# A decoder step's cross-attention: the samples' softmaxes done earlier, and the sums of squares in four column groups

## The chip, the cores and the metric

The kernel is one program on one core of a Trainium2 chip. The metric is device time in microseconds (us) of one execution. Names of engines: PE is TensorE (matmuls and transposes), DVE is VectorE, ACT is ScalarE, POOL is GpSimd, SP is SyncE, which here only issues DMAs. PEld is PE's weight load. All data are float32.

## What is computed

Two layers of a decoder run for 256 prompt tokens (one sequence) and 32 sample tokens (8 sequences of 4 tokens), 288 tokens in all, with 1024 features. Each layer is three sub-layers, each followed by `x <- LN(ALPHA*x + f(x))`: a mixer (block-sparse attention with a convolution in layer 0, a gated spatial unit in layer 1), cross-attention over 256 memory tokens, and 16 experts of which each token takes two. What the change touches is the cross-attention and the layer norm:

```python
def layer_norm(x, g, b):
    mu = jnp.mean(xf, -1, keepdims=True)
    var = jnp.mean(jnp.square(xf - mu), -1, keepdims=True)
    return (xf - mu) * lax.rsqrt(var + LN_EPS) * g + b

def cross_attn(x, mk, mv, wq, wo):          # 4 heads of 256 features
    q = (x @ wq).reshape(B, L, H_X, HD_X)
    s = jnp.einsum('blhd,bmhd->bhlm', q, mk) * (HD_X ** -0.5)
    p = jax.nn.softmax(s, axis=-1)
    o = jnp.einsum('bhlm,bmhd->blhd', p, mv).reshape(B, L, D_MODEL)
    return o @ wo
```

The prompt's memory keys and values are computed from `mem_prompt`, and are outputs too. Each of the 8 sample sequences has keys and values of its own, read from a cache in HBM (2 MB per unit of four sequences and half the data, 8 units in a layer).

## The kernel before

Tokens lie along the free dimension: a feature tile is 128 partitions by 288 tokens, eight of them a tensor. The work of every engine is written out by hand in one order, and semaphores tie the engines together. A table, `tile_order()`, lists every tile that PE writes into the four general PSUM banks (`acc`) and who empties it ("v" DVE, "s" ACT; a capital letter marks the first half of a pair copied at once). A tile's bank is its place in that table modulo 4, and PE may write it when the tile four places earlier has been emptied (`bank_free`). Three further tiles of PSUM stand outside: `psS` (scores), `psV` and `psN` (value products). SP loads 2 MB units into a ring of six slots; a unit is loaded when the one that had its slot has been read.

Cross-attention, function `cross(l)` on PE, goes through these steps. Line numbers are those of the profile.

1. Mean of the mixer's result, sum of squares, query projection `xq`, prompt scores `xs`.
2. The key loop, eight steps: `turn_keys(i)` turns 16 blocks of cached keys (L1036), DVE and ACT copy them out in pairs (L1355 on DVE, L1332 on ACT), `key_scores(i)` multiplies them with the queries into `psS` (L730). Steps 0 to 3 serve sample group 0 (sequences 0 to 3), steps 4 to 7 group 1. After step 5 come the prompt's turned probabilities and value products (`xpt`, L1083, and `xpo`), copied out by DVE at L1426 and L1428.
3. The tail, for each group g: the softmax of `psS[:, g]` (`mem_softmax`: maximum L1675 and its negation L1676 on DVE, exponential L2078 on ACT, reciprocal L1678 and scaling L1679 on DVE), the turning of the probabilities on PE (L1056) and their copy on DVE (L1680), the value products of two units into `psV` and `psN` (16 matmuls of 32x512, so 32 records), their copies (L2083 on ACT, L1686 on DVE), their turning (L1072), and eight small copies into the mixed tensor (L1692). Between the two groups stands `memory_key_rows` (L1103), which turns the prompt's keys into rows for the output. In all, PE's order is values(0), memory_key_rows(), values(1).
4. The output projection `xo` (64 matmuls), the residual (L1608), the mean, the sum of squares, and the rest of the norm.

The mean is taken "by quarters" (`mean_by_quarters`): eight matmuls with 32 columns of ones go to four column groups of the PE array, so that four partial sums stand in four quarters of the partitions. DVE copies that tile to `std` (L1584, times 32), and one matmul with a full square of ones adds the quarters and spreads the sum over all partitions. The sum of squares is taken by `mean_tile`: eight full matmuls with ones, one after another, read by DVE at L1594 (`rstd`). ACT makes the squares (L2014) from the centred values of DVE (L1589), then takes the root (L1988); DVE takes the reciprocal (L1597) and scales (L1615), ACT adds the bias (L2020).

After the tail of a layer come the router and the expert stage. Its weights (6 MB an expert, three experts held at a time) are loaded while experts are computed: a set is loaded when the expert that held its place has been used, the first three before the stage begins. Results go to HBM in small stores (L2235), two chunks deep, and DVE may fill a buffer (L1844) when the store before last out of it has landed.

Of the kernel before, what the change touches and what calls it, by code (L numbers as in the profile page):

```python
# [129 lines left out]
def tile_order():  # L130
# [49 lines left out]
    for l in range(DEPTH):  # L180
        if l:
# [4 lines left out]
            t.append((f"mv{l}", 1, "s"))  # L186
            add("vvar", 1, "v")
# [8 lines left out]
        t.append((f"mv{l}", 2 + l, "s"))  # L196
        add(f"var{3 * l}", 1, "v")
# [23 lines left out]
        if l + 1 < DEPTH:  # L221
            add(f"memT{l + 1}", 8, "vs")
        add(f"var{3 * l + 1}", 1, "v")
# [18 lines left out]
def build(nc, x_prompt, x_sample, cache_k, cache_v, state_conv, cache_mem_k, cache_mem_v, page_table,  # L242
# [17 lines left out]
    with ExitStack() as ctx:  # L260
# [68 lines left out]
        XPTS = view(512, 2, 128)  # L329
# [398 lines left out]
        def _(pe):  # L728
# [25 lines left out]
            def mean_by_quarters(stage, zz, ready):  # L754
# [250 lines left out]
            def cross(l):  # L1005
                nth = 3 * l + 1
                mean_by_quarters(f"mean{3 * l}", zT, lambda k: evacuated(pe, f"o{l}", k))

                memory_values(l, (2 + l,))
                mean_tile(f"var{3 * l}", mixT, ones_d[:, :], 8, lambda k: pe.wait_ge(squared, 4 * turn_of(3 * l) + k // 2 + 1))  # L1010
# [41 lines left out]
                def values(g):  # L1052
# [4 lines left out]
                    last.then_inc(acc_full, 1)  # L1057
                    evacuated(pe, f"xspt{l}{g}", 0)
                    for t in range(2):
# [3 lines left out]
                        for half in range(2):  # L1063
                            for b4 in range(4):
                                last = mm((psV, psN)[half][32 * b4:32 * b4 + 32, :], XPTS[:, t, 32 * b4:32 * b4 + 32],
                                          V[:, b4, 512 * half:512 * half + 512], t == 0, t == 1)
                        last.then_inc(values_used, 1)
                    pe.wait_ge(xpv_ready, 2 * (2 * l + g) + 2)
# [39 lines left out]
                for i in range(XSTEPS):  # L1108
# [14 lines left out]
                mean_by_quarters(f"mean{nth}", zT, lambda k: evacuated(pe, f"xo{l}", k))  # L1123
                if l + 1 < DEPTH:
                    memory_turned(l + 1)
                mean_tile(f"var{nth}", mixT, ones_d[:, :], 8, lambda k: pe.wait_ge(squared, 4 * turn_of(nth) + k // 2 + 1))
# [139 lines left out]
            for l in range(DEPTH):  # L1266
                if l:
# [4 lines left out]
                    mean_by_quarters("vmean", vT, lambda k: evacuated(pe, "vv", k))  # L1272
                    memory_values(l, (1,))
                    mean_tile("vvar", mixT, ones_d[:, :], 8, lambda k: pe.wait_ge(sq_v, k // 2 + 1))
# [158 lines left out]
        def _(dve):  # L1433
# [145 lines left out]

            def center(stage, zz, n, done, step):  # L1580

                if n == 8:
                    full(dve, stage + "p", 0)
                    dve.tensor_scalar(std[:, :], ACC(stage + "p", 0)[:, 0:NTOK], 32.0, None, ALU.mult)\  # L1584
                        .then_inc(emptied["v"], 1)
# [6 lines left out]
            def rstd(stage, signal_std, count):  # L1592
                full(dve, stage, 0)
# [24 lines left out]
            for l in range(DEPTH):  # L1618
# [54 lines left out]
                def mem_softmax(g):  # L1673
                    dve.wait_ge(xk_read, 8 * l + 4 * g + 4)
                    link(dve.tensor_reduce(st[:, 64:65], psS[:, g, 0:256], X, ALU.max))  # L1675
                    dve.tensor_scalar(st[:, 65 + g:66 + g], st[:, 64:65], -1.0, None, ALU.mult).then_inc(negmax, 1)  # L1676
                    dve.wait_ge(exp_done, ex + g + 1)
                    link(dve.reciprocal(st[:, 70:71], st[:, 68 + g:69 + g]))  # L1678
                    dve.tensor_scalar(XP[:, g, :], XP[:, g, :], st[:, 70:71], None, ALU.mult).then_inc(probs, 1)  # L1679
                    evac(dve, "v", f"xspt{l}{g}", 1, lambda i, a: dve.tensor_copy(  # L1680
                        XPTS, a[:, 0:256].rearrange("p (t m) -> p t m", t=2)))

                def mem_rows(g):

                    dve.wait_ge(values_used, 8 + 4 * l + 2 * g + 2)
                    dve.tensor_copy(XPV[:, 1, :], psN[:, :]).then_inc(xpv_ready, 1)  # L1686
                    for half in range(2):
# [614 lines left out]
```

## Time and profile before

| | us |
|---|---|
| median of 3 runs | 1340.78 |
| lowest and highest of them | 1337.69, 1354.15 |
| the profiled execution, its own time | 1333.24 |
| its span | 1331.6 |
| PE busy in the span | 1145.9 |
| DVE busy | 415.9 |
| ACT busy | 265.5 |

The rest of a profiled execution's time (1.64 us) lies around the span. The profile names instructions by line and by tensor; on PE most of them have the line of the helper `mm` (L730), so they are told apart by their operands and shapes. A PE group's count is of records: a float32 matmul has two, a transpose one. In a timeline row, what stands in brackets is how long the engine sat idle before the group and what released it. PEclk is the clock that was granted to TensorE, as a share of its full speed: 1.00 is 2.4 GHz and 0.50 is 1.2 GHz.

### The profile page before, as it was taken

The numbers are of one execution on the slowest core, as the hardware profiler recorded it, in microseconds if no ns is written. First come the engines' busy times: TensorE is split into PE (matmuls) and PEld (weight loads), VectorE is DVE, ScalarE is ACT, GpSimd is POOL, SyncE is SP. The second block draws the span as 40 slices with busy tenths as digits, with TensorE's granted clock in tenths as the row PEclk, the third lists the DMA queues.
The fourth block names the chain that finished last, engine by engine and source line by source line (L and its number), as shares of the span: only waits on it lengthen the run. The fifth ranks groups of instructions, "written<-read, shape, count | busy, mean of one in ns | idle before, by whom it ended". The sixth has DMA issues, their size and how long they took to land.

```text
span 1331.6 us, 27226 instructions
## 1 busy us (share of the span) xinstructions
PE 1145.9 (86%) x10758; PEld 756.2 (57%) x10759; DVE 415.9 (31%) x1144; ACT 265.5 (20%) x541; POOL 227.6 (17%) x399
## 2 busy tenths in 40 slices
PE   6998797999998979998868999999989699998860
PEld 4677555576765745555435676667756355555430
DVE  0016562723142362222112301512432722222116
ACT  1013732112230231111101312111410411111101
POOL 2003995000000001222212100000000012222232
PEclk9999998999999989999888999999999899999985
DMA  9746879943368739799999901715679187999972
GB/s 330 262 127 190 237 220 339 388 171 126 127 233 336 288 109 421 302 403 423 425 423 391 329 0 36 284 38 215 248 273 387 73 358 308 400 393 393 425 314 80
DMA packets 102625, 360.33 MB, mean 271 GB/s; under 512 B 9639, under 2 KB 11703, under 8 KB 94362
## 3 DMA queue, kind: packets, MB, share of 16 engines
q1 hardware_dynamic: 89986, 332.68, 65.4%
q0 software_dynamic: 12432, 26.51, 5.6%
q8 instruction: 42, 0.69, 0.2%
q10 hardware_dynamic: 144, 0.28, 0.1%
q14 instruction: 21, 0.17, 0.0%
HBM read 341.48 MB, written 18.38 MB: 270 GB/s over the span
## 4 chain that ended last, share of the span: by engine, by line
PE 58%; DMA 19%; DVE 11%; issue 6%; ACT 3%; SPq 1%; POOLq 1%; POOL 1%; DVEq 0%; ACTq 0%
PE acc L730 37%; DMA by_slot<-feats 10%; PE psS L730 8%; DMA ring<-in_w_exp_down 5%; PE psV L730 4%; PE psN L730 3%; DVE feats L1454 2%; DMA feats<-in_w_exp_down 2%; PE acc L1036 2%; PE acc L845 1%; DMA ring<-in_w_in_even 1%; DMA arena<-by_slot,arena 1%; ACT arena L1332 1%; PE psN L1143 1%; ACT feats L2111 1%
## 5 line engine op out<-in xcount | busy, mean ns | idle before, releaser
L730 PE MATMUL acc<-feats,ring 128*128 128x288 f32 x1280 | 316.7, 410 | 11.3 <-DMA ring<-in_w_in_even 4.4
L730 PEld LDWEIGHTS acc<-feats,ring 128*128 128x128 f32 x1280 | 245.3, 192 | 81.3 <-issue 10.3
L2235 POOL DMA_DIRECT2D by_slot<-feats x208 | 103.8, 499 | 515.0 <-DVE feats L1844 289.2
L730 PE MATMUL psS<-ring,feats 128*32 128x256 f32 x2176 | 135.9, 406 | 37.0 <-issue 37.0
L730 PEld LDWEIGHTS psS<-ring,feats 128*32 128x32 f32 x2176 | 74.6, 117 | 87.8 <-issue 50.7
L730 PE MATMUL psS<-arena,feats 128*32 128x256 f32 x1408 | 91.1, 409 | 22.6 <-issue 22.1
L1332 ACT ACTIVATE arena<-acc 128x1024 f32<-128x1024 f32 (+6 forms) x86 | 65.4, 781 | 113.5 <-PE acc L730 35.2
L2121 ACT ACTIVATE feats<-psS 64x256 f32<-64x256 f32 x52 | 19.6, 377 | 328.2 <-PE psS L730 328.2
L730 PE MATMUL psN<-arena,feats 128*32 128x256 f32 (+1 forms) x1360 | 83.5, 379 | 1.5 <-DVE feats L1763 1.5
L1836 DVE TENSOR_TENSOR feats<-feats,psS 64x256 f32<-64x256 f32 x52 | 22.1, 425 | 193.5 <-ACT feats L2121 191.6
L730 PEld LDWEIGHTS psS<-arena,feats 128*32 128x32 f32 x1408 | 46.5, 117 | 57.0 <-issue 33.7
L730 PE MATMUL psV<-ring,feats 128*32 128x256 f32 x1088 | 65.8, 382 | 0.9 <-DVE feats L1838 0.8
L1844 DVE COPY feats<-psV 128x256 f32 (+1 forms) x52 | 22.1, 425 | 132.1 <-DMA by_slot<-feats 91.5
L730 PEld LDWEIGHTS psN<-arena,feats 128*32 128x32 f32 x1360 | 44.4, 112 | 29.7 <-issue 3.2
L730 PE MATMUL acc<-arena,ring 128*128 128x256 f32 x256 | 56.2, 380 | 1.7 <-ACT arena L1332 0.9
L730 PE MATMUL acc<-ring,arena 128*128 128x512 f32 x128 | 56.2, 592 | 0.0
L1454 DVE SCALAR_TENSOR_TENSOR feats<-arena,cparT,feats 128x256 f32<-128x256 f32 (+1 forms) x180 | 55.6, 389 | 0.0
L730 PEld LDWEIGHTS acc<-arena,ring 128*128 128x128 f32 x256 | 48.4, 190 | 8.6 <-issue 2.1
L1608 DVE SCALAR_TENSOR_TENSOR feats<-feats,acc 128x288 f32<-128x288 f32 x32 | 14.5, 454 | 115.3 <-PE acc L730 115.3
L730 PEld LDWEIGHTS psV<-ring,feats 128*32 128x32 f32 x1088 | 31.9, 109 | 24.5 <-DVE feats L1838 7.0
L730 PE MATMUL acc<-arena 128*128 128x256 f32 (+6 forms) x174 | 33.7, 356 | 13.1 <-DVE arena L1420 5.6
L2014 ACT ACTIVATE feats<-feats 128x576 f32<-128x576 f32 x16 | 10.7, 683 | 151.4 <-DVE feats L1589 151.4
(344 smaller groups left out, 1243.3 us busy)
## 6 DMA issues: line engine op xcount, KB each, us to landing
ring<-in_w_exp_gate SPq DMA_DIRECT2D x22, 2048.0 KB, 14.7
ring<-in_w_exp_up SPq DMA_DIRECT2D x22, 2048.0 KB, 18.8
ring<-in_w_exp_down SPq DMA_DIRECT2D x22, 2048.0 KB, 23.7
arena<-in_w_exp_gate SPq DMA_DIRECT2D x10, 2048.0 KB, 14.9
arena<-in_w_exp_up SPq DMA_DIRECT2D x10, 2048.0 KB, 18.8
feats<-in_w_exp_down SPq DMA_DIRECT2D x10, 2048.0 KB, 23.7
ring<-in_cache_k SPq DMA_DIRECT2D x64, 256.0 KB, 3.0
ring<-in_cache_v SPq DMA_DIRECT2D x64, 256.0 KB, 3.1
```

Source lines behind the costliest of these rows:

```text
L730: return pe.matmul(out, lhsT, rhs, start=first, stop=last)
L845: last = pe.transpose(ACC("kt", 4 * i + b4)[:, 256 * f + P * t:256 * f + P * t + P], K[:, 2 * b4 + t, at:at + P], ident)
L1036: last = pe.transpose(ACC(f"xkt{l}", 4 * i + b4)[:, 256 * f + P * t:256 * f + P * t + P], K[:, b4, t, at:at + P], ident)
L1143: last = pe.transpose(psN[:, P * j:P * j + P], XR[:, P * j:P * j + P], ident)
L1332: return lambda out, in_: eng.activation(out, in_, ACT.Copy)
L1454: ins = dve.scalar_tensor_tensor(out=y, in0=u, scalar=tap, in1=y, op0=ALU.mult, op1=ALU.add)
L1608: dve.scalar_tensor_tensor(out=zT[:, i, :], in0=xT[:, i, :], scalar=ALPHA, in1=ACC(stage, i)[:, 0:NTOK], op0=ALU.mult, op1=ALU.add).then_i ...
L1836: dve.tensor_tensor(H[64:128, :], SG[64:128, :], psS[64:128, 0, 0:256], ALU.mult).then_inc(S.h, 1)
L1844: dve.tensor_copy(to, psV[:, 0:256]).then_inc(S.y, 1)
L2111: act.activation(XR, psN[:, 0:256], ACT.Copy).then_inc(S.rows_out, 1)
L2121: act.activation(SG[64:128, :], psS[0:64, 0, 0:256], ACT.Silu).then_inc(S.silu, 1)
L2235: pool.dma_start(by_slot[rows, 256 * q:256 * q + 256], YS[32 * q:32 * q + 32, at]).then_inc(S.stored, 16)
```

## The change

Four things change.

- `mean_by_quarters` becomes `sum_by_quarters`, and the sum of squares goes through it as well, at five places: `var0`, `var1`, `var3`, `var4` (the norms after each mixer and each cross-attention; layer 1's have numbers 3 and 4) and `vvar` (the gated unit's norm). The convolution's `cvar` stays as it was. DVE gets a function `quarters(stage)` that copies the partial sums to `std`, which `rstd` now calls first.
- The tail's order on PE: the probabilities' turning is a step of its own (`turn_probs`), and so is the turning of the value products (`turn_values`). The order is turn_probs(0), memory_key_rows(), values(0), turn_probs(1), turn_values(0), values(1), turn_values(1).
- The softmax is cut in pieces on DVE (`mem_maxima`, `mem_scale`, `mem_turned`; `mem_rows` and `mem_mixed` for what follows). Group 0's stands in the key loop: its maximum after the copy of step 4, its scaling after that of step 6. Group 1's maximum and scaling stand around the copies of the prompt's key rows. ACT's exponentials move accordingly.
- The turned probabilities get a buffer for each group (`XPTS[0]`, `XPTS[1]`).

```diff
@@ tile_order
+            add("vvarp", 1, "v")
             add("vvar", 1, "v")
...
         add(f"xspt{l}0", 1, "v")
-        add(f"xpvt{l}0", 2, "v")
         add(f"mktok{l}", 4, "vvss")
         add(f"xspt{l}1", 1, "v")
+        add(f"xpvt{l}0", 2, "v")
         add(f"xpvt{l}1", 2, "v")
...
-        XPTS = view(512, 2, 128)
+        XPTS = [view(512, 2, 128), view(1792, 2, 128)]
@@ PE, cross(l); var1, var4 and vvar likewise
-                mean_tile(f"var{3 * l}", mixT, ones_d[:, :], 8, lambda k: ...)
+                sum_by_quarters(f"var{3 * l}", mixT, lambda k: ...)
...
+                turn_probs(0)
+                memory_key_rows()
                 values(0)
-                memory_key_rows()
+                turn_probs(1)
+                turn_values(0)
                 values(1)
+                turn_values(1)
@@ DVE
+            def quarters(stage):
+                full(dve, stage + "p", 0)
+                dve.tensor_scalar(std[:, :], ACC(stage + "p", 0)[:, 0:NTOK], 32.0, None, ALU.mult)\
+                    .then_inc(emptied["v"], 1)
...
             def rstd(stage, signal_std, count):
+                if stage != "cvar":
+                    quarters(stage)
                 full(dve, stage, 0)
...
-                for i in range(MEMORY_VALUES_AFTER - 1, MEMORY_VALUES_AFTER + 2):
-                    cm["xkt"](l, i)
+                cm["xkt"](l, 4)
+                mem_maxima(0)
+                cm["xkt"](l, 5)
+                cm["xkt"](l, 6)
+                mem_scale(0)
                 ptpo(dve, "v", XPTPO, l)
-                cm["xkt"](l, MEMORY_VALUES_AFTER + 2)
-                mem_softmax(0)
+                cm["xkt"](l, 7)
+                mem_turned(0)
+                mem_maxima(1)
+                cm["mktok"](l)
+                mem_scale(1)
                 mem_rows(0)
-                cm["mktok"](l)
-                mem_softmax(1)
+                mem_turned(1)
+                mem_mixed(0)
                 mem_rows(1)
+                mem_mixed(1)
@@ ACT
-                for i in range(MEMORY_VALUES_AFTER + 2):
+                for i in range(6):
                     cm["xkt"](l, i)
+                mem_softmax(0)
+                cm["xkt"](l, 6)
                 ptpo(act, "s", XPTPO, l)
-                cm["xkt"](l, MEMORY_VALUES_AFTER + 2)
-                mem_softmax(0)
-                mem_rows(0)
-                cm["mktok"](l)
+                cm["xkt"](l, 7)
                 mem_softmax(1)
+                cm["mktok"](l)
+                mem_rows(0)
                 mem_rows(1)
```

How the instructions move, at three places. First PE, the tail of layer 0, from the last turned keys on; before (L1036 turned keys, psS their products, L1056 turned probabilities, psV and psN value products, L1072 their turning, L1103 the prompt's key rows):

```order
L1036 MATMUL acc<-cst,ring 128x128 x16
L730 MATMUL psS<-arena 32x256 x16
L1056 MATMUL acc<-cst,arena 128x128 x2
L730 MATMUL psV<-ring,arena 32x512 x4
L730 MATMUL psN<-ring,arena 32x512 x4
L730 MATMUL psV<-ring,arena 32x512 x4
L730 MATMUL psN<-ring,arena 32x512 x4
L1072 MATMUL acc<-cst,arena 128x128 x8
L1103 MATMUL acc<-cst,arena 128x128 x16
L1056 MATMUL acc<-cst,arena 128x128 x2
L730 MATMUL psV<-ring,arena 32x512 x4
```

and in the changed kernel (lines 3 to 10 higher, L1060, L1113 and L1082 for the same steps):

```order
L1039 MATMUL acc<-cst,ring 128x128 x16
L733 MATMUL psS<-arena 32x256 x16
L1060 MATMUL acc<-cst,arena 128x128 x2
L1113 MATMUL acc<-cst,arena 128x128 x16
L733 MATMUL psV<-ring,arena 32x512 x4
L733 MATMUL psN<-ring,arena 32x512 x4
L733 MATMUL psV<-ring,arena 32x512 x4
L733 MATMUL psN<-ring,arena 32x512 x4
L1060 MATMUL acc<-cst,arena 128x128 x2
L1082 MATMUL acc<-cst,arena 128x128 x8
L733 MATMUL psV<-ring,arena 32x512 x4
```

The key rows have moved ahead of the first value products, and the second turning of probabilities ahead of the turning of the first products.

Then DVE in layer 0, from the fifth key copy (`xkt`, step 4) to the copy of step 7; before (L1355 keys, L1426 and L1428 prompt probabilities and products, L1675 on the softmax of group 0):

```order
L1355 COPY arena<-acc 128x1024 x3
L1426 COPY arena<-acc 128x512
L1428 COPY feats<-acc 128x2x256
L1426 COPY arena<-acc 128x512
L1428 COPY feats<-acc 128x2x256
L1355 COPY arena<-acc 128x1024
L1675 TENSOR_REDUCE st<-psS 128x1
L1676 TENSOR_SCALAR st<-st 128x1
L1678 RECIPROCAL st<-st 128x1
L1679 TENSOR_SCALAR arena<-arena,st 128x256
```

and in the changed kernel (L1369, L1440, L1442 for the copies, L1696 and L1697 the maximum and its negation, L1702 and L1703 the reciprocal and the scaling):

```order
L1369 COPY arena<-acc 128x1024
L1696 TENSOR_REDUCE st<-psS 128x1
L1697 TENSOR_SCALAR st<-st 128x1
L1369 COPY arena<-acc 128x1024 x2
L1702 RECIPROCAL st<-st 128x1
L1703 TENSOR_SCALAR arena<-arena,st 128x256
L1440 COPY arena<-acc 128x512
L1442 COPY feats<-acc 128x2x256
L1440 COPY arena<-acc 128x512
L1442 COPY feats<-acc 128x2x256
L1369 COPY arena<-acc 128x1024
L1707 COPY arena<-acc 128x256
```

The maximum now stands after the first of these copies, the reciprocal and the scaling ahead of the prompt's copies, and the copy of the turned probabilities (L1707) follows the last key copy at once.

Last PE after the first cross-attention: mean, memory transposes, sum of squares, memory keys, router; before:

```order
L730 MATMUL acc<-feats,ones_d 32x288 x8
L730 MATMUL acc<-std,ones_d 128x288
L960 MATMUL acc<-cst,arena 128x128 x16
L730 MATMUL acc<-feats,ones_d 128x288 x8
L730 MATMUL acc<-arena,ring 128x256 x16
L730 MATMUL acc<-feats,wrt 32x288 x8
```

and in the changed kernel:

```order
L733 MATMUL acc<-feats,ones_d 32x288 x8
L733 MATMUL acc<-std,ones_d 128x288
L963 MATMUL acc<-cst,arena 128x128 x16
L733 MATMUL acc<-feats,ones_d 32x288 x8
L733 MATMUL acc<-std,ones_d 128x288
L733 MATMUL acc<-arena,ring 128x256 x16
L733 MATMUL acc<-feats,wrt 32x288 x8
```

The eight full matmuls on the squares have become eight of 32 columns and one full one.

## Rows read from the trace of the kernel before

**Rows 1.** The page's part 4, whole program: shares of the chain that ended last
```profile
PE 58%; DMA 19%; DVE 11%; issue 6%; ACT 3%; SPq 1%; POOLq 1%; POOL 1%; DVEq 0%; ACTq 0%
```

**Rows 2.** The same chain in order of time: start us, us, what; the first expert stage
```profile
620.05 30.03 DMA feats<-in_w_exp_down
```

**Rows 3.** Timeline, second cross-attention's end: start us, us, engine, line, operation, [idle before <-releaser]
```profile
975.04 0.41 DVE L1675 TENSOR_REDUCE st<-psS 128x1 f32<-128x256 f32 x1
...
975.27 1.07 PE L730 MATMUL psS<-arena 128*32 128x256 f32 x16 [0.41 <-DVE arena L1355]
...
976.27 0.16 DVE L1678 RECIPROCAL st<-st 128x1 f32<-128x1 f32 x1 [0.63 <-ACT arena L2078]
976.47 0.35 DVE L1679 TENSOR_SCALAR arena<-arena,st 128x256 f32<-128x256 f32 x1
...
976.97 0.41 PE L1056 MATMUL acc<-cst,arena 128*128 128x128 f32 x2 [0.63 <-DVE arena L1679]
...
977.90 1.07 PE L730 MATMUL psV<-ring,arena 128*32 128x512 f32 x8 [0.52 <-DVE arena L1680]
...
981.61 0.69 DVE L1686 COPY arena<-psN 128x512 f32<-128x512 f32 x1 [3.76 <-PE psN L730]
...
982.35 1.10 PE L1072 MATMUL acc<-cst,arena 128*128 128x128 f32 x8 [0.81 <-DVE arena L1686]
...
983.28 1.91 PE L1103 MATMUL acc<-cst,arena 128*128 128x128 f32 x16
...
987.13 0.41 PE L1056 MATMUL acc<-cst,arena 128*128 128x128 f32 x2 [1.93 <-DVE arena L1679]
...
991.76 0.69 DVE L1686 COPY arena<-psN 128x512 f32<-128x512 f32 x1 [3.76 <-PE psN L730]
...
992.51 1.09 PE L1072 MATMUL acc<-cst,arena 128*128 128x128 f32 x8 [0.81 <-DVE arena L1686]
```

**Rows 4.** Windows: bounds us, length, busy time of each engine, PEclk (granted), DMA share, GB/s
```profile
410.40:413.70 3.30, 3.30 (x20) 0.87 (x16) 0.00 (x0) 0.00 (x0) 0.00 (x0) 0.50 0.98 406
```

**Rows 5.** Timeline, second cross-attention, where the key loop gives way to prompt values
```profile
958.81 1.23 DVE L1355 COPY arena<-acc 128x1024 f32<-128x1024 f32 x1 [1.19 <-PE acc L1036]
...
960.83 1.02 ACT L1332 ACTIVATE arena<-acc 128x1024 f32<-128x1024 f32 x1 [2.06 <-PE acc L1036]
...
963.29 0.69 DVE L1426 COPY arena<-acc 128x512 f32<-128x512 f32 x1 [0.37 <-PE acc L1083]
...
964.09 1.97 PE L730 MATMUL acc<-arena 128*128 128x256 f32 x8 [0.39 <-DVE arena L1426]
```

**Rows 6.** Timeline, first normalisation: the mean by quarters, then the sum of squares
```profile
304.64 1.29 PE L730 MATMUL acc<-feats,ones_d 128*32 128x288 f32 x16
...
304.75 0.45 DVE L1608 SCALAR_TENSOR_TENSOR feats<-feats,acc 128x288 f32<-128x288 f32 x1 [3.43 <-PE acc L730]
...
307.14 7.03 PE L730 MATMUL acc<-ring,arena 128*128 128x512 f32 x16
307.34 2.75 DVE L1589 TENSOR_TENSOR feats<-feats,acc 128x576 f32<-128x576 f32 x4 [0.84 <-PE acc L730]
...
314.00 4.04 PE L730 MATMUL acc<-feats,ones_d 128*128 128x288 f32 x16
...
317.88 1.45 PE L730 MATMUL acc<-ring,arena 128*128 128x512 f32 x3
318.08 0.46 DVE L1594 TENSOR_SCALAR rs<-acc 128x288 f32<-128x288 f32 x1 [8.00 <-PE acc L730]
```

**Rows 7.** Timeline, the sum of squares after the first cross-attention
```profile
456.52 4.80 PE L730 MATMUL acc<-feats,ones_d 128*128 128x288 f32 x16
```

**Rows 8.** Timeline, the same after the second cross-attention: squares, sum, first use
```profile
1029.07 2.67 ACT L2014 ACTIVATE feats<-feats 128x576 f32<-128x576 f32 x4 [36.71 <-DVE feats L1589]
...
1034.05 0.46 DVE L1594 TENSOR_SCALAR rs<-acc 128x288 f32<-128x288 f32 x1 [3.02 <-PE acc L730]
```

**Rows 9.** Waits of DVE, second expert stage (1066 to 1300): waiter <- releaser: us, times, longest
```profile
DVE feats L1844 <- DMA by_slot<-feats: 80.2, 19, 7.2
```

More of the change, by code:

```diff
@@ L751, in mean_tile, with sum_by_quarters @@
                 last.then_inc(acc_full, 1)
-            def mean_by_quarters(stage, zz, ready):
+            def sum_by_quarters(stage, zz, ready):
                 bank_free(pe, stage + "p", 0)
@@ L1006, in cross @@
                 nth = 3 * l + 1
-                mean_by_quarters(f"mean{3 * l}", zT, lambda k: evacuated(pe, f"o{l}", k))
+                sum_by_quarters(f"mean{3 * l}", zT, lambda k: evacuated(pe, f"o{l}", k))
                 memory_values(l, (2 + l,))
-                mean_tile(f"var{3 * l}", mixT, ones_d[:, :], 8, lambda k: pe.wait_ge(squared, 4 * turn_of(3 * l) + k // 2 + 1))
+                sum_by_quarters(f"var{3 * l}", mixT, lambda k: pe.wait_ge(squared, 4 * turn_of(3 * l) + k // 2 + 1))
                 if l == 0:
@@ L1050, in key_scores, with turn_probs @@
                     last.then_inc(xk_read, 1)
-                def values(g):
+                def turn_probs(g):
                     bank_free(pe, f"xspt{l}{g}", 0)
@@ L1057, in values @@
                     last.then_inc(acc_full, 1)
+                def values(g):
                     evacuated(pe, f"xspt{l}{g}", 0)
@@ L1064, in values, with turn_values @@
                             for b4 in range(4):
-                                last = mm((psV, psN)[half][32 * b4:32 * b4 + 32, :], XPTS[:, t, 32 * b4:32 * b4 + 32],
+                                last = mm((psV, psN)[half][32 * b4:32 * b4 + 32, :], XPTS[g][:, t, 32 * b4:32 * b4 + 32],
                                           V[:, b4, 512 * half:512 * half + 512], t == 0, t == 1)
                         last.then_inc(values_used, 1)
+                def turn_values(g):
                     pe.wait_ge(xpv_ready, 2 * (2 * l + g) + 2)
@@ L1271, in _ @@
                         project("vv", UIDX["in_odd", 2 + n], xT, 4 * n)
-                    mean_by_quarters("vmean", vT, lambda k: evacuated(pe, "vv", k))
+                    sum_by_quarters("vmean", vT, lambda k: evacuated(pe, "vv", k))
                     memory_values(l, (1,))
-                    mean_tile("vvar", mixT, ones_d[:, :], 8, lambda k: pe.wait_ge(sq_v, k // 2 + 1))
+                    sum_by_quarters("vvar", mixT, lambda k: pe.wait_ge(sq_v, k // 2 + 1))
                     memory_values(l, (2,))
@@ L1592, in rstd @@
             def rstd(stage, signal_std, count):
+                if stage != "cvar":
+                    quarters(stage)
                 full(dve, stage, 0)
```

20 lines of the change are left out of this document (11 added, 9 removed).

## The prediction

> **What bounds the kernel now.** I read the page's chain of waits first: more than half of what ended last is PE's work, the rest DMA, DVE and small waits [rows 1]. So a wait or a matmul taken off PE counts wherever PE stands on that chain. Next the chain in order of time: between the expert stages it stays on PE and on the short exchanges of PE with DVE and ACT, and inside them it goes over to transfers, as the 30.03 us on one expert's weights show [rows 2]. Then the timeline of the stretches that the change touches: the two tails of the cross-attention, the end of the key loop, and the five sums of squares.
>
> The tail is a chain of single steps. In layer 1 the last key products start at 975.27 and run 1.07 us, and the output projection starts at 994.37 [rows 3]: 18.03 us from 976.34. The reader should see that PE stands still before almost every step: 0.63 us for the scaling, 0.52 for the copy of the turned probabilities, 0.81 for the copy of the products, and 1.93 for the second softmax, after the key rows [rows 3]. The norm is another chain, in which the full sum takes 4.08 us from its first matmul to its first reader (314.00 to 318.08), and the mean by quarters 2.70 us (304.64 to 307.34) [rows 6].
>
> **The change, part by part.** *The tails.* With the softmax of group 0 out of the way, PE's steps from 976.34 on follow one another. Turned probabilities of group 0: two transposes, by the key rows' 16 in 1.91 us [rows 3] 0.24 us. Key rows: 1.91. Products of group 0: 3.71 (977.90 to the copy at 981.61). Their copy until the turning starts: 0.74 (981.61 to 982.35). Turning until the next group of matmuls: 0.93 (982.35 to 983.28). Products of group 1, the same 16 matmuls: 3.71 again. Copy: 0.75 (991.76 to 992.51). Turning, small copies, projection: 1.86 (992.51 to 994.37). All from [rows 3], the sum is 13.85, against 18.03: 4.18 us less.
>
> What is costed at nothing there, and its cover: the copy of group 0's turned probabilities and group 1's maximum (0.41), negation, exponential, reciprocal (0.16) and scaling (0.35) [rows 3] lie under the key rows and the first products, 5.6 us together, in which DVE has besides them only two key-row copies. The second turning of probabilities (0.24) lies under the copy of the products on DVE and ACT, and its own copy, queued behind that one on DVE, under the turning of the products. If the second softmax weren't ready, the products' turning would wait behind it on PE, up to the 1.93 us of [rows 3].
>
> *The key loop* pays for group 0. Its maximum and negation stand after the key copy of step 4; DVE sits idle 1.19 us before the next copy [rows 5], so they fit. ACT's exponential stands before a copy that waited 2.06 us [rows 5]: it fits. The reciprocal and scaling don't. The copy before them ends at about 962.93, the prompt's copy starts at 963.29, and PE waits for it (0.39) [rows 5]. 0.16 + 0.35 and the hand-over between them, some 0.6 us, into a gap of 0.36: 0.25 us late, and PE with it. Net of a tail: 4.18 - 0.25 = 3.93 us, for both layers 7.9.
>
> *The clock in layer 0's tail.* From 410.40 to 413.70, in the second value products, the granted clock was 0.50 (1.2 GHz); it cost half of 3.30, so 1.65 us [rows 4]. Layer 1's same step ran at its 3.71 [rows 3]. The change packs PE's steps closer, so this may go: 1.65 at best, 0 if it stays, and a loss of as much if layer 1 catches one. I take 1.0, since two tails of one shape show that it isn't bound to the shape.
>
> *The sums of squares.* Where PE starts the sum late, behind other matmuls, the whole length counts. To the next group on PE it is 3.88 us now (314.00 to 317.88) and 2.50 by quarters (304.64 to 307.14); to the reader on DVE 4.08 and 2.70 [rows 6]. Both give 1.38 us, with the added DVE copy to `std` inside. Three places are like this (var0, vvar and var3, each behind a block of memory values): 4.1 us. At var0 and vvar a further block of memory values follows on PE, but since PE's and the norm's parts both move by 1.38, so does what waits for both. var1 took 4.80 us [rows 7] instead of 4.04: between 1.38 and 4.80 - 2.50 = 2.3 us; I take 2.0, since the excess is clock and fewer matmuls meet it. At var4 nothing lies ahead of it: ACT's last square ends at 1031.74 and the reader starts at 1034.05 [rows 8]. By quarters, from the last input (305.20) to the reader (307.34) it is 2.14 us [rows 6], so 1033.9: 0.15 us. Sum: 4.1 + 2.0 + 0.15 = 6.3.
>
> This is where a page is weighed. The trace's figures for the quarters include the copy, and it is the larger half: of 2.70 us the matmuls take 1.29 [rows 6]. The Trainium skill, TensorEngine Tiling, section PSUM Bottleneck, says that tiling speeds up TensorE and not the evacuation, and that the copy may then become the bottleneck. Taken as the rule for all five places, it would make the 6.3 nothing. By the rows it holds at var4 alone, the place where the squares come last.
>
> *Queues.* SP's loads gated on the value products, on var1 and on the last turning are issued up to 6 us earlier, into stretches with room. The stores of the prompt's key rows go out earlier too. The projection's second weight unit is loaded once the last keys are turned, just before the tail begins, and has 13.85 us plus half a projection instead of 18 plus that: costed at nothing; if it were late, each us counts.
>
> *Passing on.* Both tails and the norms lie ahead of an expert stage. That stage is bound by transfers in part, but its loads, all except the first three experts', start when an expert has been used, so the whole stage moves with its start. I let the gain pass in full.
>
> Sum: 7.9 + 1.0 + 6.3 = 15.2 us. Against the profiled execution's own 1333.24 that is 1318; it lies 7.5 under the median, and below all three runs. Against the median of 1340.78 it is 1325.6. The medians are what is compared, but three runs 16 us apart place theirs poorly; I take 1323.
>
> **The rivals.**
>
> *The quarters give nothing* (the page's rule, as a mechanism of this kernel): each sum's end is set by squares or by DVE's copy. For it: var4, and one more exchange at each place. Against it: at var0 PE starts at 314.00, and DVE's centring, which the squares follow piece by piece, runs from 307.34 for 2.75 us, to 310.09 [rows 6]. 6 us lost: 1329. Chance 0.08.
>
> *The clock takes it back.* Each sum now has a wait of PE in its middle, and a half-clock stretch costs 1.65 us [rows 4]. Five such stretches more: 8 us, so 1331. For it: var1 comes after a chain of short exchanges and is already slow [rows 7]. Against it: the mean has the same wait in its middle, and the sum behind it runs its 16 records in 4.04 us, without the excess of var1 [rows 6]. [...] Chance 0.08.
>
> *The expert stages keep the gain.* Their transfers are late or early by more than it, as the three runs' 16 us suggest: 1337, no difference to be seen. Chance 0.12.
>
> *Slower: the small stores of layer 1's expert stage.* DVE waits there 80.2 us in 19 waits for stores to land, the longest 7.2 [rows 9]. The change shifts the phase between stores and weight loads. From 15.2 / 19 = 0.8 us more a wait the change is a loss; halfway from the mean 4.2 to the longest, 1.5 us more, it is 28 us, so 1351. For it: the waits vary much already. Against it: nothing in the stage itself changes, and a shift can as well shorten them. Chance 0.06, of which 0.02 beyond 2%.
>
> *The change doesn't do what it says:* the second softmax isn't ready, or products of one group wait for the other's copies, so that a tail keeps its waits: half of the 7.9 goes, 1327. Chance 0.06.
>
> **How the numbers follow.** My forecast has the remaining 0.60, with a range of its own of 1312 to 1331 (1318 and 1325.6, and 6 us for the clock, var1 and the runs' spread). Taking in the rivals at 1329, 1331, 1327 and 1337, and some of the upper one's start, I set 1309 to 1337 for 8 in 10. Within 2% of 1340.78, about what a measurement of this kernel can tell from no change, is 1314 to 1368: the forecast's lower tail below 1314 is 0.10, the store rival above is 0.02, the rest 0.88.
>
> **What would show it.** In the profile after: from the end of the last key products to the projection 14 us in both layers, with no PE wait above 0.9 us; group 1's scaling finished before the first products end; PE's wait before the prompt's first products some 0.6 us instead of 0.39; the sums of squares 2.7 us from first matmul to reader at var0, vvar and var3, and no gain at var4; the clock at 1.00 through layer 0's second products; expert stages as long as before. It is wrong if the tails still show a wait for a softmax, if the projection waits for its weights, or if the stages' length moves by more than some 5 us.

## The result, and the profile after

| | before | changed |
|---|---|---|
| median, runs taken together (6 each) | 1342.36 | 1326.01 |
| lowest and highest of the changed kernel | | 1321.15, 1333.92 |
| ratio, with its 95% interval | | 0.9898 [0.9864, 0.9933] |
| the profiled execution, its own time | 1333.24 | 1324.23 |
| its span | 1331.6 | 1322.6 |
| its mean granted clock | 0.954 | 0.948 |

The changed kernel is about 1% faster, and 1326.01 lies in the range of 1309 to 1337, 3 us above the 1323 that was forecast. The chain of waits is made up as in [rows 1]: PE still has 58% of it and DMA 19%, with DVE at 10% and issue at 7% in place of 11% and 6%.

The tail of layer 0 in the changed kernel, timeline (start us, us, engine, line, operation, [idle before <-releaser]). It answers to [rows 3], which are layer 1's of before; layer 1's of the changed kernel has the same steps.

```profile
395.17 1.07 PE L733 MATMUL psS<-arena 128*32 128x256 f32 x16 [0.41 <-DVE arena L1369]
396.17 0.44 PE L1060 MATMUL acc<-cst,arena 128*128 128x128 f32 x2
396.44 1.91 PE L1113 MATMUL acc<-cst,arena 128*128 128x128 f32 x16
398.28 1.06 PE L733 MATMUL psV<-ring,arena 128*32 128x512 f32 x8
...
398.91 0.35 DVE L1703 TENSOR_SCALAR arena<-arena,st 128x256 f32<-128x256 f32 x1
...
401.85 0.44 PE L1060 MATMUL acc<-cst,arena 128*128 128x128 f32 x2
401.99 0.69 DVE L1713 COPY arena<-psN 128x512 f32<-128x512 f32 x1 [2.73 <-PE psN L733]
402.74 1.10 PE L1082 MATMUL acc<-cst,arena 128*128 128x128 f32 x8 [0.45 <-DVE arena L1713]
403.76 1.07 PE L733 MATMUL psV<-ring,arena 128*32 128x512 f32 x8
...
408.22 1.09 PE L1082 MATMUL acc<-cst,arena 128*128 128x128 f32 x8 [0.81 <-DVE arena L1713]
410.08 15.27 PE L733 MATMUL acc<-feats,ring 128*128 128x288 f32 x62 [0.77 <-DVE feats L1722]
```

Of PE's waits for a softmax none is left. Group 1's probabilities are scaled by 399.26, 2.6 us before their turning at 401.85. From the end of the last key products (395.17 + 1.07 = 396.24) to the projection (410.08) it is 13.84 us. The end of the tail in [rows 3], the projection in layer 1 of before:

```profile
994.37 7.03 PE L730 MATMUL acc<-feats,ring 128*128 128x288 f32 x28 [0.77 <-DVE feats L1692]
```

The first sum of squares (`var0`) in the changed kernel, timeline. It answers to the full sum in [rows 6].

```profile
314.46 1.18 PE L733 MATMUL acc<-feats,ones_d 128*32 128x288 f32 x16
...
315.71 0.46 DVE L1597 TENSOR_SCALAR std<-acc 128x288 f32<-128x288 f32 x1 [5.26 <-PE acc L733]
316.22 0.75 PE L733 MATMUL acc<-std,ones_d 128*128 128x288 f32 x2 [0.58 <-DVE std L1597]
316.81 2.74 PE L733 MATMUL acc<-ring,arena 128*128 128x512 f32 x6
317.01 0.46 DVE L1614 TENSOR_SCALAR rs<-acc 128x288 f32<-128x288 f32 x1 [0.84 <-PE acc L733]
```

From the sum's first matmul it is 2.55 us to the reader instead of 4.08, and 2.35 to PE's next group instead of 3.88: 1.53 us. The sum itself starts 0.10 us later behind the block before it (6.96 us after that block's start instead of 6.86), so 1.43 reaches the next group.

**Where it came from and where it stopped.** Differences between the starts of the same groups in the two profiled executions make an account. Won: 1.43 at `var0`, 0.44 in the key loop, 5.89 in layer 0's tail, 1.65 at `var1`, 1.44 each at `vvar` and `var3`, 0.61 from layer 1's query projection to the end of its key loop (0.45 of it in the loop), 4.19 in its tail, 0.22 at `var4`; about 17.3 together. Given back: 0.36 before `var0`; 1.56 and 2.31 between the router and the first expert, in layer 0 and layer 1; 2.75 in the first expert stage; 0.09 in layer 1's mixer; 1.24 in the second expert stage and at the end; about 8.3. That leaves the 9.0 us by which the two spans differ.

The two stretches from the router's first matmul to the first expert's first product, windows (bounds us, length, busy us of PE, PEld, DVE, ACT, POOL, granted clock, DMA share, GB/s). Before:

```profile
468.16:485.85 17.69, 11.08 (x91) 7.37 (x91) 11.72 (x45) 8.52 (x13) 0.00 (x0) 0.79 0.32 122
1038.24:1057.84 19.60, 13.11 (x91) 7.84 (x91) 13.90 (x51) 10.64 (x18) 0.00 (x0) 0.83 0.15 59
```

Changed:

```profile
459.11:478.36 19.25, 12.53 (x92) 8.79 (x91) 11.83 (x45) 8.44 (x13) 0.00 (x0) 0.71 0.29 112
1025.69:1047.60 21.91, 15.84 (x90) 9.97 (x91) 13.89 (x51) 10.62 (x18) 0.00 (x0) 0.66 0.14 58
```

The same work took longer at a lower granted clock: PE busy rose by 1.4 and 2.7 us, DVE and ACT didn't move. In the expert stage, the chain's step of [rows 2] and the next of its kind, in the changed kernel, in order of time:

```profile
612.39 31.95 DMA feats<-in_w_exp_down
673.81 31.95 DMA ring<-in_w_exp_down
```

The first was 30.03 and is 1.9 us longer, the second was 32.45. DVE's waits for stores in the second expert stage, to be held against [rows 9]:

```profile
DVE feats L1881 <- DMA by_slot<-feats: 82.3, 19, 7.2
```

2 us more over 19 waits, and the same longest one: the rival of the stores didn't come. The projection after the tail in layer 1 took 31.21 us to the next mean in both kernels, so its second weight unit wasn't late either.

### The profile page after: what moved, and what is told of

Read it like the earlier page. It is cut to its first block, busy times and chain, and to the rows that moved or that the text cites. A ratio compares the mean times of both kernels' runs of the same rounds, so it can differ in the third digit from the quotient of the medians.

```text
span 1322.6 us, 27256 instructions
## 1 busy us (share of the span) xinstructions
PE 1139.5 (86%) x10768; PEld 746.4 (56%) x10769; DVE 417.7 (32%) x1149; ACT 265.4 (20%) x541; POOL 226.4 (17%) x399
## 4 chain that ended last, share of the span: by engine, by line
PE 58%; DMA 19%; DVE 10%; issue 7%; ACT 3%; SPq 1%; POOLq 1%; POOL 1%; DVEq 0%; ACTq 0%
PE acc L733 37%; DMA by_slot<-feats 10%; PE psS L733 8%; DMA ring<-in_w_exp_down 5%; PE psV L733 4%; PE psN L733 3%; DVE feats L1468 2%; DMA feats<-in_w_exp_down 2%; PE acc L1039 2%; PE acc L848 1%; DMA ring<-in_w_in_even 1%; DMA arena<-by_slot,arena 1%; PE psN L1157 1%; ACT arena L1346 1%; ACT feats L2148 1%
## 5 line engine op out<-in xcount | busy, mean ns | idle before, releaser
L733 PE MATMUL psS<-ring,feats 128*32 128x256 f32 x2176 | 138.8, 412 | 40.1 <-issue 38.8
L2158 ACT ACTIVATE feats<-psS 64x256 f32<-64x256 f32 x52 | 19.6, 377 | 333.5 <-PE psS L733 333.5
L1873 DVE TENSOR_TENSOR feats<-feats,psS 64x256 f32<-64x256 f32 x52 | 22.1, 425 | 195.2 <-ACT feats L2158 194.3
L1881 DVE COPY feats<-psV 128x256 f32 (+1 forms) x52 | 22.1, 425 | 134.9 <-DMA by_slot<-feats 95.8
## 6 DMA issues: line engine op xcount, KB each, us to landing
arena<-in_w_exp_up SPq DMA_DIRECT2D x10, 2048.0 KB, 19.5
```

What stands on the lines that cost most here:

```text
L733: return pe.matmul(out, lhsT, rhs, start=first, stop=last)
L1873: dve.tensor_tensor(H[64:128, :], SG[64:128, :], psS[64:128, 0, 0:256], ALU.mult).then_inc(S.h, 1)
L1881: dve.tensor_copy(to, psV[:, 0:256]).then_inc(S.y, 1)
L2158: act.activation(SG[64:128, :], psS[0:64, 0, 0:256], ACT.Silu).then_inc(S.silu, 1)
```

## The experiments

My theory after the traces: the tails and the sums each give what was summed, and they add up; the profiled execution of the changed kernel lost clock that the one of before had kept, mainly where PE waits in short exchanges. The rival: one of the two parts gives nothing and the other more.

### One part each

The tails alone: the five sums again as eight full matmuls.

```diff
-                sum_by_quarters(f"var{3 * l}", mixT, lambda k: ...)
+                mean_tile(f"var{3 * l}", mixT, ones_d[:, :], 8, lambda k: ...)
...   (vvar and var of the norms after cross-attention likewise)
-                if stage != "cvar":
-                    quarters(stage)
```

> The changed tails stay, the five sums of squares are again eight full matmuls. Theory: the parts add up, each at its own place. In the profile the sums take 4.1 us to their first reader at var0, vvar and var3, and the tails 13.8 us as in the changed kernel; ahead of the second expert stage the kernel has won 10 to 11 of the 17 us that the changed kernel wins there. The time lies 6 us above the changed kernel's, so 9 to 11 us under the kernel before (ratio 0.992). Rival, that the two parts hide one another's waits: then this kernel is as fast as the changed one, ratio 0.990. Rival, that the time is made by the granted clock and not by the steps: then the ratio follows the mean granted clock of its runs, whatever the steps do.

Measured: 1330.46 us, median of 11 runs; ratio 0.9904 [0.9871, 0.9937]. Both tails took 13.84 us in its trace. The ratio lies at the 0.990 of the rival that the parts hide one another's waits, and can't be told from the changed kernel's first 0.9898; the sums alone, and the changed kernel measured again, have to decide.

The sums alone: the kernel before with the five sums by quarters.

```diff
-                mean_tile(f"var{3 * l}", mixT, ones_d[:, :], 8, lambda k: ...)
+                mean_by_quarters(f"var{3 * l}", mixT, lambda k: ...)
...   (the others, their partial tiles in tile_order and DVE's copy likewise)
```

> The five sums of squares go by quarters, the cross-attention's tails are as before. Theory: 1.4 to 1.5 us are won at var0, vvar and var3, 2.0 at var1, 0.2 at var4, together 6 to 7 us ahead of the second expert stage, and the tails take 18.0 us (up to 1.7 more where a half-clock stretch falls into one). The time is 1342 - 6 = 1336 us, ratio 0.995. If the rule that the copy becomes the bottleneck held, each sum would end no earlier than before, and the ratio would be 1.000.

Measured: 1334.20 us, 12 runs; 0.995 [0.991, 0.999]. Both parts give something, so the rival that one of them gives nothing falls. Their product is 0.9854; the changed kernel was measured at 0.9898 first, so it was run once more, unaltered, beside the kernels with fillers (below).

> The changed kernel once more, beside the kernels with fillers on one chip, and for more runs of it. Theory: the time of a run follows the array time lost to the half clock, (1 - mean granted clock) x time, with about 0.75 us a lost us, and at equal loss it lies 15 to 16 us under the kernel before; ratio 0.989 to 0.991. Rival: the earlier session favoured it by chance, and its ratio is nearer to 0.985, the product of the two halves' ratios.

Measured: 1326.89 us, 6 runs; 0.9860 [0.9820, 0.9901]. This is at the product: the ratio of 0.989 to 0.991 that I expected was missed, and the rival's 0.985 came. The two measurements of the changed kernel overlap, so the parts add within what can be told. The ratios by themselves are too wide to show it; the fit further down, at equal loss of clock, puts the tails alone 7.6 and 10.2 us above the changed kernel's two sets.

### The second softmax late again

The order of PE stays, but group 1's maximum, exponential and scaling stand behind the copies of group 0's products.

```diff
@@ DVE
-                mem_maxima(1)
                 cm["mktok"](l)
-                mem_scale(1)
                 mem_rows(0)
+                mem_maxima(1)
+                mem_scale(1)
                 mem_turned(1)
@@ ACT
-                mem_softmax(1)
                 cm["mktok"](l)
                 mem_rows(0)
+                mem_softmax(1)
```

> The changed kernel, but group 1's maximum, exponential and scaling stand on DVE and ACT behind the copy of group 0's value products, as they would if they weren't ready. Theory: PE's turned probabilities of group 1 wait behind maximum, negation, exponential, reciprocal and scaling, and the turning of group 0's products waits behind them, so each tail is 1.6 to 2.2 us longer (13.8 to about 15.7 us), 3 to 4 us in both layers. Rival, that the order of PE alone makes the gain (key rows ahead of the products): then the tails stay at 13.8 us.

Its trace, layer 0's tail:

```profile
404.89 0.41 DVE L1696 TENSOR_REDUCE st<-psS 128x1 f32<-128x256 f32 x1
...
406.32 0.35 DVE L1703 TENSOR_SCALAR arena<-arena,st 128x256 f32<-128x256 f32 x1
...
406.82 0.41 PE L1060 MATMUL acc<-cst,arena 128*128 128x128 f32 x2 [2.61 <-DVE arena L1703]
```

PE waits 2.61 us for the scaling, in both layers. The tail is 15.82 us in layer 1, so 1.98 longer than 13.84, and 17.47 in layer 0, where the turning of the first products and the second products also ran partly at half clock. Measured: 1332.97 us, 12 runs; 0.9933 [0.9897, 0.9969], 6 to 7 us over the changed kernel's two medians. The direct cost is 4.0 us in two tails, as expected; the rest goes together with a lower clock: its runs had 0.941 on average, the changed kernel's 0.946 and 0.943. Of the 4.19 us that layer 1's tail won, 1.98 hang on having group 1's softmax early. The other 2.21 (18.03 to 15.82) stay without it, so they come from PE's order and group 0's early softmax, which no run separates.

### PE kept busy in its waits

If the half clock after short exchanges is what took the gain back, matmuls whose result nobody reads, put into PE's waits, must bring it back. They leave the output as it is. A first try used 512 columns:

```diff
+            def warm(n):
+                for _ in range(n):
+                    mm(psV[:, :], ones_d[:, :], cst[:, 0:512], True, True)
...   (8 before layer 1's query projection, 3 and 8 around its last sum, 1 before the
...    router's sums, 5 before the ranks, 1, 1 and 2 around the first expert's turning)
```

> The changed kernel with matmuls of ones on constants, whose result nobody reads, put into PE's waits: eight after the last sum of squares of layer 1 and eight before its query projection, three before layer 1's last sum, and ten in each layer's router and expert set-up. Theory: what the changed kernel lost again between router and first expert (1.9 us in layer 0, 2.3 in layer 1) is the clock at half speed in short steps with waits. With the waits filled the granted clock stays at 1.00 there, the half-clock stretches at 446 to 485, 893 to 898 and 1023 to 1051 us go, and 4 to 8 us with them: about 1320 us, mean granted clock up by 0.006 or more. Rival: the fillers themselves stand in the way, since a filler at half clock takes 0.86 us instead of 0.43, and the time is the same or up to 5 us longer while the clock still falls.

Measured: 1323.85 us, 6 runs; 0.9861 [0.9808, 0.9913]; mean clock 0.960. The low clock went, but one filler took 0.86 us, twice what I had meant, so that 8 of them ran 7.03 us in a wait of 4.2: the query projection started 2.5 us later after the last sum, and won back 1.6 by its clock (31.20 us instead of 32.80). Against the changed kernel's two medians it is 2 to 3 us, and not the 4 to 8 expected. The next version has fillers of 256 columns (`mm(psV[:, 0:256], ident, cst[:, 0:256], True, True)`, 0.43 us each), in numbers that fit the waits: 8 before layer 1's query projection, 3 and 8 around its last sum, and 2, 5, 1 and 3 from the router's sums to the first expert, in each layer.

> The changed kernel with fillers half as long as those of the first try (256 columns, 0.43 us each at full clock) and counted to fit the waits: eight before layer 1's query projection, three before and eight after its last sum, and eleven in each layer's router and expert set-up, none between the first picking and its turning. Theory: the first fillers overran their waits by 2 to 3 us at three or four places and still won, so with the overrun gone the stretches router to first expert stay at 1.00 of the clock and the kernel gains 4 to 9 us on the changed one: 1317 to 1322 us, ratio 0.982 to 0.985. Rival: short fillers leave the clock to fall as it does without them, and the ratio stays at 0.990.

Measured: 1321.24 us, 6 runs; 0.982 [0.9779, 0.9860], as expected. All six (1316.58 to 1323.57) lie below all six of the changed kernel measured beside them (1324.31 to 1331.03). The same with 32 more of them in earlier stages (6 behind the prompt's scores of the first mixer, 10 before its first output product, 3 before the first turned memory, 8 before the second sample values, 5 before the convolution's mean):

> The same with fillers in the attention part as well: six after the prompt's scores, ten before its first value product, three before the memory is turned, eight before the second group's sample values, five before the convolution's mean. Theory: the half-clock stretches at 127 to 135, 164 to 172, 202 to 210, 226 to 234 and 257 to 261 us go, 15 us of lost array time, and where PE is on the chain of waits there that is worth 4 to 9 us on top: 1310 to 1317 us, ratio 0.976 to 0.981. Rival: in that part DVE and ACT set the end (softmax and convolution), a faster PE waits longer for them, and nothing is won beyond the sized fillers.

Measured: **1313.56 us**, 6 runs, 1311.95 to 1324.53; 0.9777 [0.9731, 0.9823]. This is the fastest version, faster than both kernels, 2.2% under the one before, and in the expected range. What each of the five new places gives wasn't taken apart. And the kernel before with the fillers of the second version and no other change:

> The kernel before (old tails, full sums of squares) with the sized fillers at the same places. Theory: the clock's part has nothing to do with the change, and the kernel before wins from them as well, somewhat less than the changed one since its router stretches lost 5.1 and 5.1 us of array time and not 8.5 and 10.2: 3 to 6 us, ratio 0.9955 to 0.998. Rival: only the changed kernel suffers in those stretches, and this ratio is 1.000.

Measured: 1334.81 us, 12 runs; 0.9925 [0.9889, 0.9960]. The median is 11.1 us lower, where 3 to 6 were expected: the clock costs the kernel before as well. It won more from the fillers than the changed kernel (5.7), against the theory that the changed one has more to win back. With them in both, the two are 13.6 us apart, without them 19.0 beside the same runs; why is open.

The router stretches of the fastest version, windows as above:

```profile
456.95:474.20 17.25, 15.35 (x113) 10.71 (x113) 11.69 (x45) 8.54 (x13) 0.00 (x0) 0.90 0.34 124
1020.10:1039.48 19.38, 16.27 (x113) 10.80 (x113) 13.93 (x51) 10.76 (x18) 0.00 (x0) 1.00 0.15 61
```

There are 21 and 23 more records on PE in them (the eleven fillers are 22), and yet they are 2.00 and 2.53 us shorter than the changed kernel's. The rows of layer 1, first in the changed kernel, timeline of PE:

```profile
1025.69 4.08 PE L733 MATMUL acc<-feats,wrt 128*32 128x288 f32 x16 [4.23 <-ACT feats L2057]
...
1037.62 1.43 PE L733 MATMUL acc<-arena 128*128 128x16 f32 x6 [2.78 <-DVE arena L1791]
...
1042.34 2.79 PE L733 MATMUL psN<-arena,feats 128*32 128x256 f32 x24 [0.73 <-DVE feats L1800]
...
1047.60 5.17 PE L733 MATMUL psS<-ring,feats 128*32 128x256 f32 x64 [1.29 <-ACT feats L2150]
```

and in the fastest version:

```profile
1015.72 3.62 PE L733 MATMUL psV<-cst 128*128 128x256 f32 x16
1020.10 3.59 PE L733 MATMUL acc<-feats,wrt 128*32 128x288 f32 x16 [0.77 <-ACT feats L2077]
...
1028.45 2.32 PE L733 MATMUL psV<-cst 128*128 128x256 f32 x10
1031.31 0.81 PE L733 MATMUL acc<-arena 128*128 128x16 f32 x6 [0.54 <-issue]
...
1034.10 1.50 PE L733 MATMUL psN<-arena,feats 128*32 128x256 f32 x24
...
1039.48 3.66 PE L733 MATMUL psS<-ring,feats 128*32 128x256 f32 x64 [1.63 <-issue]
```

The fillers (the rows `psV<-cst`) lie in the waits of 4.23 and 2.78 us. The router's 16 records take 3.59 us instead of 4.08, at a granted clock of 1.00 instead of 0.50; most of their length isn't clock in either, as they follow ACT's eight instructions on their inputs (3.54 us in both). The small matmuls that follow take 0.81 instead of 1.43, the 24 records after them 1.50 instead of 2.79, the first expert's 64 3.66 instead of 5.17.

### The same stretches in all traces

The table is from one trace of each kernel: the tails (end of the last key products to the projection), and the stretch from the router to the first expert, for layer 0 and layer 1.

| kernel | tails | router to expert |
|---|---|---|
| before | 19.73, 18.03 | 17.69, 19.60 |
| sums only | 19.41, 19.72 | 19.24, 19.50 |
| tails only | 13.84, 13.84 | 18.03, 21.86 |
| changed | 13.84, 13.84 | 19.25, 21.91 |
| changed, again | 13.84, 13.84 | 19.25, 21.95 |
| changed, second softmax late | 17.47, 15.82 | 19.10, 22.11 |
| before, sized fillers | 18.04, 19.73 | 17.25, 19.45 |
| changed, first fillers | 13.84, 13.84 | 18.66, 18.33 |
| changed, sized fillers | 13.84, 13.84 | 17.26, 19.34 |
| changed, more fillers | 13.84, 13.93 | 17.25, 19.38 |

Old tails come in 18.03 and, with a half-clock stretch, in up to 19.73, in four of six cases. New ones came in 13.84 in eleven of twelve (the twelfth 13.93), but with the second softmax late, and PE waiting 2.61 us for it, one of two had a half-clock stretch again. The router stretch of layer 0 is longer wherever the sums are by quarters and no fillers stand there (19.1 to 19.3, against 17.7 and 18.0), the one of layer 1 wherever the order of the tails is new (21.9 to 22.1, against 19.5 and 19.6). With the sized fillers both are at 17.25 and 19.4, whatever the kernel. Why a sum or a tail so far ahead should matter there, no run shows.

### What a run's clock explains

The second trace of the changed kernel has a span of 1329.4 against 1322.6. The same 48 matmuls in both, timeline, first trace:

```profile
837.65 7.84 PE L733 MATMUL acc<-arena 128*128 128x128 f32 x48 [1.18 <-ACT arena L1346]
```

second trace:

```profile
836.52 12.30 PE L733 MATMUL acc<-arena 128*128 128x128 f32 x48 [1.09 <-ACT arena L1346]
```

4.46 us for nothing but clock; PEclk over the 28 us around it is 1.00 in the first and 0.70 in the second. Lost array time is (1 - mean granted clock) x time of a run. Over all 92 runs without fillers (those of before in two sets, of the changed kernel in two, and of three experiments), time follows it with 0.76 us a us within each set, correlations 0.73 to 0.96. Put at the same loss of 70 us, the kernel before stands at 1341.3 and 1342.5, tails only at 1333.1 (8.2 less than its set), sums only at 1331.6 (9.7 less), and the changed kernel at 1325.5 and 1322.9, so 15.8 and 19.6 less. This is a fit, not an experiment: the filler runs are the experiment, and there 22 us less of lost array time (75.9 to 53.9) brought 5.7 us, since part of the lost time lies where PE waits anyway and the fillers cost some.

## Why the prediction was right

- *The tails.* The step "the sum is 13.85" measured 13.84, in both layers. 4.18 a layer was 4.19, by the layer that had no clock loss before. The cover held: group 1's softmax was done 2.6 us before its turning.
- *The key loop.* "0.25 us late, and PE with it" was wrong, and 0.5 of the 15.2 us with it: nothing was late. I had queued the reciprocal and scaling of group 0 behind the end of the copy before them. In the trace of the changed kernel:

```profile
381.61 1.23 DVE L1369 COPY arena<-acc 128x1024 f32<-128x1024 f32 x1 [1.67 <-PE acc L1039]
...
382.75 0.15 DVE L1702 RECIPROCAL st<-st 128x1 f32<-128x1 f32 x1
382.94 0.35 DVE L1703 TENSOR_SCALAR arena<-arena,st 128x256 f32<-128x256 f32 x1
383.20 0.68 DVE L1440 COPY arena<-acc 128x512 f32<-128x512 f32 x1
...
383.99 1.97 PE L733 MATMUL acc<-arena 128*128 128x256 f32 x8 [0.39 <-DVE arena L1440]
```

  The reciprocal starts 0.09 us before the copy's end (382.84) and the prompt's copy 0.09 before the scaling's; between reciprocal and scaling lie 0.04 us. From the start of the one to the prompt's copy it is 0.45 us, and with the overlap they fit the gap of 0.36 that was there before. PE's wait stays 0.39, as in [rows 5].
- *The key loop's start*, which I had not named, gave 0.44 and 0.45 us. `vvarp`, `var0p` and the like add tiles to the table that gives each its bank, so the first turned keys meet other banks. Before, in layer 0:

```profile
362.70 1.14 PE L1036 MATMUL acc<-cst,ring 128*128 128x128 f32 x8
364.90 2.07 PE L1036 MATMUL acc<-cst,ring 128*128 128x128 f32 x16 [1.07 <-ACT arena L2069]
```

  and in the changed kernel:

```profile
361.62 1.47 PE L1039 MATMUL acc<-cst,ring 128*128 128x128 f32 x12
363.83 0.66 PE L1039 MATMUL acc<-cst,ring 128*128 128x128 f32 x4 [0.73 <-ACT arena L2106]
```

  PE turns 12 before a wait of 0.73 instead of 8 before one of 1.07. With the tails alone it is 8 and 1.07, with the sums alone 12 and 0.73: this gain came with the sums, and their added tiles. That it is the banks is read from the table, no run changed them alone.
- *The clock in layer 0's tail.* I took 1.0 of at most 1.65; the stretch went whole, 1.7 us. That it went was more than luck: by the table above such a stretch came in four of six old tails and in none of the new ones that had the softmax in time. The layer it falls in isn't fixed: in the trace of the kernel before it was layer 0, in the one with fillers layer 1, and with the sums alone both.
- *The sums.* 1.38 was to come at three places. From the first matmul to PE's next group it was 1.53, and since each sum starts 0.1 us later behind its block, 1.43 to 1.44 reached what follows. At `var1` 2.0 was 1.95 from the first matmul to the reader, and 1.65 at the router. At `var4` 0.15 was 0.22:

```profile
1016.74 2.68 ACT L2051 ACTIVATE feats<-feats 128x576 f32<-128x576 f32 x4 [36.71 <-DVE feats L1607]
1017.56 2.58 PE L733 MATMUL acc<-feats,ones_d 128*32 128x288 f32 x16 [1.65 <-ACT feats L2051]
...
1021.50 0.46 DVE L1614 TENSOR_SCALAR rs<-acc 128x288 f32<-128x288 f32 x1 [0.85 <-PE acc L733]
```

  ACT's squares end at 1019.42, and the matmuls follow them: PE's part is stretched to 2.58 us by waiting for squares. The Trainium skill, TensorEngine Tiling, section PSUM Bottleneck, says that tiling speeds up TensorE and not the evacuation, and that the copy may become the bottleneck. At `var4` little was won, but by the squares and not by the copy; at the other four the copy of 0.46 us didn't take up the gain, and the quarters kept 1.4 us and more.
- *Passing on.* "I let the gain pass in full" is the step that failed for the profiled executions: 17.3 us were won, 2 more than the 15.2 summed, and 9.0 stood at the end. 3.9 went between router and first expert by the clock. The fillers show that: with them the stretches are back at their length. 2.75 went in the first expert stage (1.9 in one transfer, 0.5 won back in the next), and 1.24 in the second and at the end; no run took those apart. For the medians it held: they lie 16.4 us apart in the first measurement (13.7 by its ratio) and 19.0 in the second. The profiled execution of before was one with little clock lost (61 us of array time; its sets had 71 and 75 on average), the changed kernel's less so (69; its sets 72 and 76), so that two single executions understate the change. Over all runs the two kernels lost as much array time as each other (72 and 76 us against 71 and 75), and the sized fillers gave the kernel before 11.1 us and the changed one 5.7. So "the changed kernel loses clock that the other keeps" is true of the two profiled executions, and not of the kernels.
- *The rival of the clock* had the right mechanism at another place. The sums themselves ran at full clock but for the start of `var1`'s (1.51 us for the 16 records that take 1.18 at `var0`); the long exchanges of the router behind them did not. Its price, 3.9 us in the profiled execution, was half of the 8 us. The Trainium skill, TensorE: Matmul & The Clock Gate, section HAM oscillation, describes TensorE falling back to the lower clock when it waits between bursts. The rows of the router stretch agree: PE was idle for 4.23 us, and the 4.08 us of the router's 16 records behind that wait had a granted clock of 0.50; with fillers in the wait it was 1.00.
- *The number.* 1323 lay between 1318 (against the profiled execution) and 1325.6 (against the median); 1326.01 says that the median was the better base. The sum came near it with errors that cancelled in part: the key loops won 0.9 us where 0.5 was to be lost, the clock in the tail 0.7 more than taken, and the router stretches and the expert stages gave back 7.9 us in the profiled execution. That is luck beside a right mechanism.

## What to carry to other kernels

Where PE's waits in a chain can be read one by one, a reordering can be summed closely by the steps' own rows (here 13.85 us against 13.84): take the wait away where its cause lies, and check on the other engines that what replaces it has cover. But in both traces of the changed kernel the shorter chain was followed by a lower clock in the next stage, so read the granted clock of the stages behind the change, and compare two kernels by many runs or at equal clock, not by two profiled executions (here 9.0 us apart, against 16.4 and 19.0 in the medians). Where PE waits 2 to 4 us in such exchanges, matmuls that nobody reads are worth a try: sized to end before the wait does, they gave the changed kernel 0.4% and, in more places, 1.0%, and the kernel before 0.75%; of twice the length, they overran the waits and gave no gain that could be told.

## What the hardware showed that was not expected

- Half-clock stretches are not tied to one place. In the same kernel one came in a feed of 48 matmuls (12.30 us against 7.84) in one execution and not in the other, and the spread between runs goes mostly with the clock: the changed kernel's went from 1321.15 at a mean clock of 0.950 to 1333.92 at 0.937.
- PE's busy time can rise while the kernel gets faster: 1152.7 us in the fastest version against 1139.5 in the changed kernel, at a span of 1313.0 against 1322.6.
- On DVE a [128x1] reciprocal of 0.15 us started 0.09 us before the large copy ahead of it ended, and a copy started as much before the end of the scaling ahead of it.
